# A hybrid decoder trunk on one core: sums of squares of queries and keys in two rounded passes, and a search for top values moved

## The reference

```python
def rms_norm(x, gain):
    xf = xf * lax.rsqrt(jnp.mean(xf * xf, axis=-1, keepdims=True) + NORM_EPS)
# sparse attention, per head of 64 channels
q = rope(rms_norm(q.reshape(b, L, DSA_HEADS, DSA_HEAD_DIM), q_norm), positions)
k = rope(rms_norm(k.reshape(b, L, DSA_HEADS, DSA_HEAD_DIM), k_norm), positions)
score = jnp.einsum("bqh,bqhs->bqs", wib, rel)      # indexer scores of a block of 128 queries
_, idx = lax.top_k(score, topk)                    # topk = 128
# S5 branch
g_lin, g_gate = jnp.split(y @ w_glu, 2, axis=-1)
return g_lin * jax.nn.sigmoid(g_gate)
```

## Time and profile before

| what | us |
|---|---|
| median of 3 runs | 2754.15 (2753.99 to 2754.34) |
| the profiled execution | 2754.87 |
| its span in the trace | 2753.0 |
| PE busy | 2746.3 |
| DVE busy | 1840.7 |
| ACT busy | 1331.1 |
| POOL busy | 926.6 |

### The profile page before, as it was taken

How to read it: one execution, slowest core, us unless ns; L and a number is a source line. 1 busy time by engine, 2 the same in 40 slices (tenths; PEclk the granted TensorE clock), 3 DMA queues, 4 the chain that set the end, 5 groups by cost and what they waited for, 6 DMA issues and landing times.

```text
span 2753.0 us, 41817 instructions
## 1 busy us (share of the span) xinstructions
PE 2746.3 (100%) x16054; PEld 2335.9 (85%) x16054; DVE 1840.7 (67%) x2982; ACT 1331.1 (48%) x2095; POOL 926.6 (34%) x458
## 2 busy tenths in 40 slices
PE   9999999999999999999999999999999999999999
PEld 7898888777788888898998988887777888898988
DVE  7686857785667448585785878577856674585755
ACT  6353444655355446353563534446553653553533
POOL 0134824333343442131121357243333434421221
DMA  5333583222222232233332335842222222323332
GB/s 171 107 107 116 151 181 106 78 76 70 85 85 85 85 99 94 92 116 100 108 107 92 116 115 159 169 108 79 75 74 79 86 85 85 100 95 97 108 98 102
DMA packets 113108, 284.80 MB, mean 103 GB/s; under 512 B 35616, under 2 KB 45344, under 8 KB 112416
## 3 DMA queue, kind: packets, MB, share of 16 engines
q1 hardware_dynamic: 112928, 282.35, 34.5%
HBM read 268.67 MB, written 9.44 MB: 101 GB/s over the span
## 4 chain that ended last, share of the span: by engine, by line
PE 96%; DVE 2%; DMA 1%; ACT 0%; issue 0%; SPq 0%; DVEq 0%; ACTq 0%
PE bank L618 22%; PE bank L620 21%; PE bank L619 21%; PE bank L667 7%; PE bank L668 7%; PE bank L669 7%; PE bank L644 1%; PE bank L646 1%; PE bank L645 1%; PE bank L1028 1%; PE bank L1047 1%; PE bank L1062 1%; PE bank L808 1%; PE bank L1161 1%; PE bank L1002 0%; DMA da_s<-da_qk 0%
## 5 line engine op out<-in xcount | busy, mean ns | idle before, releaser
L473 POOL TENSOR_TENSOR w_lo<-raw,w_hi 128x1024 fp32r<-128x1024 f32 x208 | 518.5, 2496 | 891.5 <-ACT w_hi L465 891.4
L618 PE MATMUL bank<-h_hi,w_hi 128*128 128x512 f32 x1504 | 593.4, 395 | 0.4 <-DVE silu_a L2326 0.3
L619 PE MATMUL bank<-h_lo,w_hi 128*128 128x512 f32 x1504 | 585.8, 390 | 0.0
L620 PE MATMUL bank<-h_hi,w_lo 128*128 128x512 f32 x1504 | 585.8, 390 | 0.0
L465 ACT ACTIVATE w_hi<-raw 128x1024 fp32r<-128x1024 f32 x310 | 326.4, 1056 | 358.7 <-PE bank L620 316.1
L538 POOL TENSOR_TENSOR w_lo<-raw,w_hi 128x1024 fp32r<-128x1024 f32 x122 | 223.4, 1852 | 802.8 <-DVE bank L2271 802.8
L618 PEld LDWEIGHTS bank<-h_hi,w_hi 128*128 128x128 f32 x1504 | 282.3, 188 | 65.1 <-issue 6.7
L620 PEld LDWEIGHTS bank<-h_hi,w_lo 128*128 128x128 f32 x1504 | 282.4, 188 | 59.8
L619 PEld LDWEIGHTS bank<-h_lo,w_hi 128*128 128x128 f32 x1504 | 282.6, 188 | 56.4
L618 PE MATMUL bank<-g_hi,w_hi 128*128 128x512 f32 x698 | 271.9, 390 | 0.0
L619 PE MATMUL bank<-g_lo,w_hi 128*128 128x512 f32 x698 | 271.6, 389 | 0.0
(11 more groups left out here) (447 smaller groups left out, 5868.2 us busy)
## 6 DMA issues: line engine op xcount, KB each, us to landing
raw<-in_w_lots SPq DMA_DIRECT2D x478, 512.0 KB, 3.7
s_wd<-s_z SPq DMA_DIRECT2D x8, 512.0 KB, 2.7
s_t<-s_taps SPq DMA_DIRECT2D x16, 256.0 KB, 13.0
da_s<-da_qk SPq DMA_DIRECT2D x16, 256.0 KB, 4.1
x<-in_x SPq DMA_DIRECT2D x8, 256.0 KB, 5.7
raw_k<-in_w_lots SPq DMA_DIRECT2D x8, 256.0 KB, 6.1
s_w_im<-s_wd SPq DMA_DIRECT2D x32, 64.0 KB, 4.3
s_w_re<-s_wd SPq DMA_DIRECT2D x32, 64.0 KB, 2.6
```

What stands on the lines that cost most here:

```text
L473: eng.tensor_tensor(w_lo[:, s], raw[:, s], w_hi[:, s].bitcast(f32), SUB).then_inc(S["lo_done"], 1)
L618: pe.matmul(b[:, :], w_hi[:, s, kw], xh[:, k], start=(k == 0), stop=False)
L619: pe.matmul(b[:, :], w_hi[:, s, kw], xl[:, k], start=False, stop=False)
L620: return pe.matmul(b[:, :], w_lo[:, s, kw], xh[:, k], start=False, stop=(k == nk - 1))
```

## The change

The diff does five things. A new step `da_high(g)` has ACT round the squares of queries (or keys) into `da_hi[g]` (four 128x512 copies), and POOL subtract them from the squares, in place, into `da_lo[g]` (four 128x512 subtractions, each waiting for its copy). In `da_norm` PE does two fp32r matmuls per tile, high and low, against a rounded block matrix `blk_r`, and waits on `da_low` in place of `da_sq`; DVE makes `blk_r` by one 128x128 copy in `s5_in`. The step for the queries stands between `da_index(2)` and `tokens("v")`; the step for the keys behind `da_index(3)`, and there ACT waits for the rotation of the same tile of the keys, since `da_hi_k` lies where `da_s` lay. The eight rounds of top values of block 1 move from between `da_rope(1, 0, 4)` and `da_index(3)` to behind `glu_end(0)`, and `glu_mul(1)` now stands ahead of `glu_end(0)`. One semaphore of the start-up code is dropped for another one's third count.

```diff
--- before.py
+++ after.py
@@ -87,8 +87,8 @@
     s += [("lot", "q", 1), ("lot", "q", 2), ("s5_in",), ("lot", "q", 3), ("lot", "k", 0), ("s5_out", 0)]
     s += [("lot", "k", 1), ("lot", "k", 2), ("s5_out", 1), ("da_square", 0), ("da_rope", 0, 0, 2), ("lot", "qi", 0), ("s5_back",)]
     s += [("s5_end",), ("lot", "qi", 1), ("da_rope", 0, 2, 4), ("lot", "k", 3), ("da_index", 1), ("da_square", 1), ("glu", 0), ("glu_mul", 0)]
-    s += [("da_index", 2), ("tokens", "v"), ("da_rope", 1, 0, 4)] + topk(1, 0, 4) + [("da_index", 3), ("glu", 1)]
-    s += [("glu_end", 0), ("glu_mul", 1)]
+    s += [("da_index", 2), ("da_high", 0), ("tokens", "v"), ("da_rope", 1, 0, 4)] + topk(1, 0, 0) + [("da_index", 3), ("da_high", 1), ("glu", 1)]
+    s += [("glu_mul", 1), ("glu_end", 0)] + topk(1, 0, 4)
     s += [("da_norm", 0), ("glu_end", 1), ("glu", 2), ("glu_mul", 2), ("da_norm", 1)]
     s += [("glu", 3), ("glu_end", 2), ("glu_mul", 3), ("m2_decay",), ("glu_end", 3)]
     fill = merges(1) + lots(("xbc", 6), ("z", 4))
@@ -337,6 +337,10 @@
         da_ki = at("da_ki", [P, SEQ], f32, 0, extra + 5 * TILE)
         da_s = at("da_s", [P, 4, SEQ], f32, A + 4)
         da_t = [at("da_tq", [P, 4, SEQ], f32, 0, extra), at("da_tk", [P, 4, SEQ], f32, A + 8)]
+        da_lo = [at("da_lo_q", [P, 4, SEQ], f32r, 0, extra), at("da_lo_k", [P, 4, SEQ], f32r, A + 8)]
+        da_hi = [[at("da_hi_q%d" % j, [P, SEQ], f32r, Y + t) for j, t in enumerate((2, 3, 6, 7))],
+                 [at("da_hi_k%d" % j, [P, SEQ], f32r, A + 4 + j) for j in range(4)]]
+        blk_r = at("blk_r", [P, P], f32r, 0, extra + 7 * TILE + 1024)
         da_r = at("da_r", [P, 4, SEQ], f32, A + 27)
         da_o = at("da_o", [P, 4, P], f32, 0, extra + 6 * TILE)
 
@@ -387,14 +391,14 @@
         MIXED = """normed_ready h_step mg_hi_done mg_done s5_in s5_step s5_args s5_powers s5_phase s5_rot
             s5_aj s5_ca_ready s5_mag_ready s5_gen s5_tap_psum s5_tap_done s5_tap_d s5_tap_out s5_w_turned s5_w_out s5_w_in
             s5_u_out s5_u_in s5_bu s5_bu_used s5_state s5_taps_in s5_y s5_y2_act s5_y2_dve s5_back s5_y_used m2_zs
-            gel_hi_done gel_done glu_y_done y_hi_done y_done small_psum small_done merge_used da_sq da_ms
+            gel_hi_done gel_done glu_y_done y_hi_done y_done small_psum small_done merge_used da_sq da_low da_ms
             da_ln da_rms da_shifted da_rope da_rot_done da_rel da_relu da_score da_logit da_max da_exp da_rec da_prob
             da_pt_psum da_pt_ready da_pv da_o_done m2_dtb m2_abs m2_dt_ready m2_acs m2_acs_sum m2_acs_hi m2_acs_lo m2_sel m2_acs_turn
             m2_acs_done m2_ct m2_xdt_done m2_conv m2_silu m2_cbp m2_cb_done m2_acb m2_seg m2_decay m2_m m2_yp m2_y m2_sq
             m2_ms m2_sum m2_rms m2_yn hg_e hg_fg hg_lf hg_cum hg_ec hg_ke hg_ket hg_ken hg_attp hg_att hg_upd hg_updu hg_turn
             hg_op hg_o hg_ex hg_sq hg_rms hg_yn hg_lc hg_el""".split()
         ONCE = """act_seq dve_seq pool_seq mix_clear c_ones c_rest c_pos x0_in_t_hi x1_in_prod x2_in_piece x3_in_xcopy x4_in x5_in_yv x6_in x7_in_t_sum w0_in_t_lo
-            p_hi p_lo p_step p_ang p_trig p_gam1 p_seq e_out""".split()
+            p_hi p_lo p_step p_ang p_trig p_seq e_out""".split()
 
         X_IN = ("x0_in_t_hi", "x1_in_prod", "x2_in_piece", "x3_in_xcopy", "x4_in", "x5_in_yv", "x6_in", "x7_in_t_sum")
         S = {}
@@ -984,6 +988,9 @@
             def glu_end(i):
                 pass
 
+            def da_high(g):
+                pass
+
             def da_square(g):
                 pass
 
@@ -998,8 +1005,9 @@
 
                     pe.wait_ge(S["da_ln"], 4)
                 for j in range(4):
-                    pe.wait_ge(S["da_sq"], 4 * g + j + 1)
-                    pe.matmul(bank[4 + j][:, :], C("blk"), da_t[g][:, j], start=True, stop=True).then_inc(S["da_ms"], 1)
+                    pe.wait_ge(S["da_low"], 4 * g + j + 1)
+                    pe.matmul(bank[4 + j][:, :], blk_r[:, :], da_hi[g][j][:, :], start=True, stop=False)
+                    pe.matmul(bank[4 + j][:, :], blk_r[:, :], da_lo[g][:, j], start=False, stop=True).then_inc(S["da_ms"], 1)
 
             def da_index(b):
 
@@ -1243,7 +1251,7 @@
                 pass
 
             STEPS = dict(lot=lot, tokens=tokens, turn_small=turn_small, out=out, out_start=out_start, glu=glu, glu_mul=glu_mul, glu_end=glu_end,
-                         gate=gate, branch=branch, merge=merge, da_square=da_square,
+                         gate=gate, branch=branch, merge=merge, da_square=da_square, da_high=da_high,
                          quad=quad, s5_in=s5_in_, s5_out=s5_out, s5_back=s5_back,
                          s5_end=s5_end, da_norm=da_norm, da_rope=da_rope, da_index=da_index, da_topk=da_topk, att_start=att_start,
                          att=att, att_end=att_end, m2_decay=m2_decay, m2_conv=m2_conv, m2_prep=m2_prep,
@@ -1519,6 +1527,12 @@
                             after(step[1], i)
                     elif step[0] in ("glu", "out"):
                         after(*step)
+                    elif step[0] == "da_high":
+                        g = step[1]
+                        for j in range(4):
+                            pool.wait_ge(S["da_sq"], 8 + 4 * g + j + 1)
+                            pool.tensor_tensor(da_lo[g][:, j], da_t[g][:, j], da_hi[g][j][:, :].bitcast(f32), SUB) \
+                                .then_inc(S["da_low"], 1)
                     elif step[0] in ("gate", "branch"):
                         after(step[0] + str(step[1]), step[2])
 
@@ -1756,7 +1770,7 @@
                 act.activation(rope_sin[:, :], ang[:, 0], AFT.Sin, scale=C("sign", 0, 1)).then_inc(S["p_trig"], 1)
                 act.activation(rope_cos[:, :], ang[:, 1], AFT.Sin, scale=-1.0, bias=half_pi[:, :]) \
                    .then_inc(S["p_trig"], 1)
-                act.wait_ge(S["p_gam1"], 1)
+                act.wait_ge(S["p_ang"], 3)
                 act.activation(gtmp[:, 1], gtmp[:, 0], AFT.Exp).then_inc(S["p_trig"], 1)
 
             def s5_prepare(phase):
@@ -1937,6 +1951,14 @@
                 act.wait_ge(S["glu_y_done"], i + 1)
                 split_y(1, i, glu_y[i % 2][:, :], scale=0.5)
 
+            def da_high(g):
+                for j in range(4):
+                    act.wait_ge(S["da_sq"], 4 * g + j + 1)
+                    if g:
+
+                        act.wait_ge(S["da_rope"], 4 + j + 1)
+                    act.activation(da_hi[g][j][:, :], da_t[g][:, j], AFT.Copy).then_inc(S["da_sq"], 1)
+
             def da_square(g):
                 if g:
 
@@ -2702,6 +2724,7 @@
                 do(TT(s5_s[:, 0, :, 1:S5_CH + 1], rows(pr[1]), rows(pr[3]), SUB))
                 do(TT(pr[0], pr[0], sn, MUL))
                 chain(TT(pr[2], pr[2], cs, MUL))
+                do(V.tensor_copy(blk_r[:, :], C("blk")))
                 TT(s5_s[:, 1, :, 1:S5_CH + 1], rows(pr[0]), rows(pr[2]), ADD).then_inc(S["s5_state"], 1)
 
             def s5_out(phase):
@@ -3067,7 +3093,7 @@
                     ins = V.tensor_tensor(gtmp[:, 0, l], gam[:, l], gtmp[:, 2, 0], SUB)
                     if l < DEPTH - 1:
                         pdo(ins)
-                ins.then_inc(S["p_gam1"], 1)
+                ins.then_inc(S["p_ang"], 1)
 
                 V.wait_ge(S["p_trig"], 3)
                 pdo(V.tensor_copy(gtmp[:, 3, 0], gtmp[:, 1, 0]))
```

## The result

| | before | after |
|---|---|---|
| median of 7 runs | 2754.19 us (2753.99 to 2754.80) | 2763.94 us (2763.32 to 2764.51) |
| profiled execution, its span | 2754.87, 2753.0 us | 2764.45, 2762.6 us |
| PE busy | 2746.3 us | 2745.0 us |
| mean granted clock of the execution | | 0.998 |

The ratio is 1.0035 with a 95% interval of 1.0025 to 1.0044. The kernel is 9.75 us slower; forecast were 2763.6 us as a median.

The account below looks back on a forecast made before the run. PE, busy 2746.3 of 2753.0 us, was taken as the bound. Against the profiled execution: 2754.87 + 6.0 (lateness, savings swallowed) + 3.4 (clock) = 2764.3 us, 2763.6 as a median; forecast's own range 2759 to 2768, chance 0.45.

Parts of the forecast that it names:

- PE's saving: Sums of a group on PE fall from 3.43 to 1.82 us: 1.6 us a group, 6.5 us for both layers.
- ACT at zero: Four 128x512 copies per group on ACT fit behind relus and cost nothing, with a margin of a few tenths.
- Collisions on DVE: POOL's eight subtractions a layer stop two-input DVE instructions, 8 x 1.03 = 8.2 us; with the long split 10.4 us.
- the long split: POOL's weight split at 490.66 us, formerly under the search, now falls on the rotation and costs DVE 2.1 us more.
- DVE's schedule: In layer 0 glu_mul(1) ends at 504.9 us, the search at 513.5, glu_mul(2) at 517.2 where it was 508.1.
- The gap: PE stands idle 6.2 us ahead of gate(1, 0) in each layer, waiting for DVE's glu_mul(2).
- Lateness per layer: From gate(1, 0) on, the rest of each layer runs 3.0 us later than before; 6.0 us in both.
- The copy for `blk_r` and the semaphore of the start-up: DVE's 128x128 copy and the moved semaphore count in the start-up each cost zero.
- The clock: After each gap PE runs at half rate for 3.4 us, losing 1.7 us a gap, 3.4 us in all; bounds 0 to 6.8.
- the two rivals in which DVE loses less: Cheaper collisions with POOL: 4.2 us lost gives 2747.6 us, chance 0.13; 6.2 us lost gives 2751.6 us, chance 0.13.

Follow-up runs that it names:

- experiment 2: The changed kernel with the search back at its old place and glu_end ahead of glu_mul, leaving the rounded sums alone: 2755.36 us, ratio 1.0003.
- experiment 8: The changed kernel with the low parts of the squares made by DVE in place of POOL: 2755.90 us, ratio 1.0007.
- experiment 4: The changed kernel with 24 matmuls whose sums nobody reads, put on PE ahead of gate(1, 0): 2759.45 us, ratio 1.0017.
- experiment 7: The changed kernel without POOL's eight subtractions a layer, PE's second pass reading the high parts again: 2757.57 us, ratio 1.0010.
- experiment 3: The kernel before with only the search moved behind glu_mul(1) as in the change, no rounding: 2754.84 us, ratio 1.0001.
- experiment 5: The changed kernel with four of the eight search rounds kept ahead of glu_mul(2) and four behind it: 2756.67 us, ratio 1.0007.

## Why the prediction was right

By its steps, in the order of the prediction:

- **PE's saving**: 1.6 us a group forecast, 1.58 and 1.56 measured (3.43 less 1.85 and 1.87). Right.
- **ACT at zero**: right, with the margin of a few tenths that was named. The last copy ended at 496.39, 0.26 us ahead of the tanh's start.
- **Collisions on DVE**: forecast 8 x 1.03 = 8.2 us and 2.1 for the long split. Against their durations alone, in the kernel before and in experiments 2 and 8, the lengthened instructions of layer 0 add up to 3.92 us beside the first four subtractions and 3.84 beside the second, and 2.15 for the split (2.89 us at 491.07 in place of 0.74): 9.9 us. Right within 0.5 us. The search under a weight split kept its 0.98 us a round (505.14 to 513.00, with POOL's 2.40 us split from 507.99), as the Trainium skill has it of instructions with one SBUF input outside DVE's two-port modes (SBUF — State Buffer, Who interferes with whom). The prediction's sentence left that exception out, and it matters: the weighing at 495.59 is a TENSOR_SCALAR with one tensor to read, and took 1.52 us beside POOL in place of 0.49.
- **DVE's schedule**: `glu_mul(1)` forecast for 504.9, ended at 504.37; search forecast to 513.5, ended at 513.0; `glu_mul(2)` forecast for 517.2, ended at 516.70. The half microsecond is mostly the one of the point above.
- **The gap**: 6.2 us forecast, 5.60 measured. Lateness per layer 3.0 forecast; 2.6 measured in layer 0 (516.85 less 514.23) and 2.7 in layer 1, 2.4 by the median of experiment 4. The copy for `blk_r` and the semaphore of the start-up, put at zero, show no cost: PE reaches the score products at 488.97 us, 488.94 before; the shift between traces hides anything under 1 us or so.
- **The clock**: 1.7 us a gap forecast, from the start of the kernel. Measured: 1.7 us in layer 0 and 2.4 in layer 1; taking the idleness away gave 4.5 to 5.0 us. The forecast's sum was 9.4 us, and 9.75 came: by the traces the lateness was 0.7 us too high (6.0 against 5.3) and the clock 0.7 too low (3.4 against 4.1), and the two errors cancel. That the total is so close is in part luck. This term rested on one analogy and was the weakest: its rows show four instructions against six in the same time, not one against two, at a PEclk of 1.00. Without experiment 4 it would only be argued.

As the Trainium skill has it (TensorE: Matmul & The Clock Gate, Part 1: The HAM clock gate), idleness sends the array to the lower clock and activity brings it back; the 5.60 us gaps of this case agree, both times.

One reading was too simple, though it did not show in the number. The prediction named POOL's collisions as the expensive part, 10.4 us. That is what they last, not what they cost. Experiment 7 takes away 7.8 of them and gets back 2.8 us a layer, since DVE would otherwise have stood waiting for ACT; experiment 3 has none of them, and `glu_mul(2)` is still 5.8 us later than before. The search's new place weighs about as much: it puts 7.9 us that lay over waits for ACT and under a weight split on the path. From the same place `glu_mul(2)` ends 5.8 us later than before with the rounding alone (2.2 of it a low part under a weight split), 5.8 with the move alone and 8.6 with both. PE's wait in layer 0 is 5.60 us with the whole change, 2.81 without POOL's work, 2.17 and 0.41 with the search at its old place, and nothing ahead of the gates with the search behind `glu_mul(2)`.

For the same reason the two rivals in which DVE loses less could not have come by their mechanism. Both let DVE run on without a wait when the collisions are cheaper; in experiment 7 there are no subtractions at all, PE still waits 2.81 us a layer, and the time is 2757.57 us, not 2747.6 or 2751.6.

Open stays what exactly chooses between slow and full rate behind a gap of 2.3 to 2.8 us. The account above gives banks by layer 0, as the text ahead of the prediction does; in layer 1 the same steps are one bank further.

## What to carry to other kernels

Work on an engine off the critical path can be cheap where it stands because it covers that engine's waits; move it, and the waits remain while the work is added. So put a movable block behind the last thing that the bottleneck engine waits for, and before pricing a collision ask what its victim would have waited for otherwise. An idle gap on TensorE cost its length and, after every gap of 3.5 us or more here, then 1.6 to 2.4 us more in half-rate passes; judge a change by the latest input at the first place where the bottleneck comes earlier.

## What the runs showed of the hardware that was not expected

- Gaps of two to three us already lower the clock, but not each time. A gap of 2.33 us was followed by 3.3 us of slow passes (experiment 2), one of 2.17 in the same execution by none; of two gaps of 2.83 us in one execution one cost 2.8 us in slow passes and the other nothing (experiment 5). Of the seven gaps of 2.33 to 2.84 us in experiments 2, 5, 7 and 8, five were followed by slow passes. After 3.48, 3.63 and 5.60 us they were there every time.
- The slow stretch need not begin with the restart: in experiment 2 the rate fell 1.0 us behind the wait's end, after passes 0.23 us apart, and in layer 1 of experiment 7 1.2 us behind it (1885.77 to 1887.00).
- The times of the kernels with gaps of 2.8 us (experiments 5, 7 and 8) spread more than the others': the middle half of their runs lies within 1.7 to 2.5 us, that of the change and of the other experiments within 0.4 to 1.1. That fits a half-rate stretch that comes in some executions and not in others; it was seen only in the profiled ones.
- The delay goes both ways between POOL and DVE: POOL's four subtractions took 5.73 and 6.31 us under DVE's instructions (single ones 1.30 to 1.74), against 4 x 1.30 by the earlier trace rows.
